# One 8 KB run per partition for the expert matrices, and the row list loaded one job ahead on GpSimd

## The chip, the core and the metric

The kernel runs on one core of a Trainium2 chip. The core has a matrix engine (TensorE, PE, with its weight loads shown as PEld), VectorE (DVE), ScalarE (ACT), GpSimd (POOL) and SyncE (SP), which here issues transfers only. Sixteen DMA engines move data between the chip's memory (HBM) and the on-chip memory of 128 partitions (SBUF). The metric is the time of one execution on the device in microseconds. Host work before the launch, such as laying out inputs anew, is not in it.

## What is computed

Two layers over 1024 latent and 256 context tokens of width 1024: a modulated attention sub-layer with three mixers, then a mixture of 32 SwiGLU experts. The change touches the second part alone:

```python
def hier_moe(h, w_rg, w_re, w_gate, w_up, w_down):
    ...                      # top-1 group of 4, then top-2 of its 8 experts, weights w
    order = jnp.argsort(flat_e)
    tok = order // TOP_K
    sizes = jnp.bincount(flat_e, length=N_EXPERTS).astype(jnp.int32)
    xs = h[tok]
    a = lax.ragged_dot(xs, w_gate, sizes)      # 1024 -> 512
    u = lax.ragged_dot(xs, w_up, sizes)        # 1024 -> 512
    y = lax.ragged_dot(jax.nn.silu(a) * u, w_down, sizes)   # 512 -> 1024
    y = y * w.reshape(-1)[order][:, None].astype(y.dtype)
    return jax.ops.segment_sum(y, tok, num_segments=n)
```

All tensors are float32. The first layer routes 1280 tokens, the second only the 1024 latent ones.

## The kernel before

A layer is four stages, each a block of programs, one for each engine: projection, attention, merge, experts. The experts stage routes the tokens, runs the experts in `run_experts`, and combines the results.

**Jobs.** `run_experts` deals the work in jobs. A job is up to 128 token rows of one expert; an expert with more rows gets more jobs. The number of jobs is data-dependent (`load_count`); the trace shows 35 in the first layer and 38 in the second. Each engine runs its own program over the jobs with a hardware loop (`Fori`), and semaphores alone tie the engines together.

**Weights.** For every job, SyncE loads the expert's three matrices, each 2 MB, in two halves of 1 MB into `raw[GATE]`, `raw[UP]` and `raw[DOWN]` (`load`, L2352; the source is written by `expert_half`, L2272). A partition's 2048 floats of a half are four rows of 512 for gate and up, and two rows of 1024 for down: since row k*128+p goes to partition p, its pieces lie 128 rows apart in HBM. A half is loaded again as soon as it has been split.

**Splitting.** The matrices are split into a rounded part and a rest, and each product is three passes. ScalarE writes the rounded part of both halves (`split`, L2410: L2415). VectorE subtracts to get the rest (L2519) for the halves of gate and up and the first half of down. GpSimd does the second half of down (`rest_of_down`, L2391: L2394). `wait_split` (L2334) is the wait for them, on TensorE and on SyncE before it reloads the half.

**TensorE** does in job g: gate (24 matmuls, L2566), up (24), the transposes of the rows of job g+1 (8, L2558), the down products of job g-1 (24, L2580), and the transposes of the hidden rows of job g (4, L2602).

**Rows.** GpSimd fetches the rows of job g+2 in `gather` (L2374): it waits until the gather before has landed, loads the list of 128 row numbers (`index`, one buffer, L2381), waits for it, waits until TensorE has transposed the rows of job g+1 (`xt`), and issues the indirect DMA that fills `x` (one buffer, L2386). After it, in the same iteration, comes `rest_of_down(g)`.

**VectorE's order** in job g (`body`, L2527) is: the two halves of gate for g+1, `hidden` of g (L2534), the rest of the transposed rows of g+1 (`rows_lo`, L2524), the two halves of up for g+1, the rest of hidden (L2539), first half of down. TensorE's gate products of g+1 wait for `rows_lo`. **ScalarE's order** (`body`, L2431) is: SiLU of g (L2435), gate of g+1, rows of g+1 (L2421), up of g+1, the result of g-1 and its store to `ye` (512 KB), hidden of g (L2443), down of g.

Of the kernel before, what the change touches and what calls it, by code (L numbers as in the profile page):

```python
# [17 lines left out]
P = 128  # L18
# [10 lines left out]
DEPTH, D, SEQ, CTX = 2, 1024, 1024, 256  # L29
# [13 lines left out]
NG, EG, NE, EH = 4, 8, 32, 512  # L43
# [22 lines left out]
def later(g, lag):  # L66


    return not isinstance(g, int) or g >= lag


def take_waits(eng, taken):


    eng.sem_inc(taken.sem, 1)
# [2196 lines left out]
def expert_half(io, l, e, n, half):  # L2272

    w = io[("w_exp_gate", "w_exp_up", "w_exp_down")[n]]
    rows = w.shape[2] // 2
    return w[l, e, half * rows:(half + 1) * rows, :].rearrange("o (k p) n -> p (o k) n", p=P)


def run_experts(nc, io, scr, l, nq, st, inner, ident, jobs, starts, more_jobs, r, scat, raw, raw_in,
# [5 lines left out]
    def sb(name, shape, dt=F32):  # L2285
        return st.sb(name, shape, dt, inner)
# [4 lines left out]
    w = [sb(f"w_{n}", [P, 2, 2, 2048], F32R) for n in ("gate", "up", "down")]  # L2291
# [23 lines left out]
    two = sb("two", [P, 2 * nq, NE])  # L2315
# [7 lines left out]
    def load_count(eng):  # L2323
        eng.wait_ge(counted.sem, counted.done(0))
        return eng.value_load(more_jobs[0:1, 0:1], min_val=0, max_val=J - NE) + NE
# [17 lines left out]
    with nc.Block() as block:  # L2343
# [27 lines left out]

        @block.gpsimd
        def _(pool):
            def gather(g):  # L2374
                if later(g, 1):
                    pool.wait_ge(x_in.sem, x_in.done(g - 1))
                if isinstance(g, int):
                    start = g * T
                else:
                    start = pool.value_load(starts[0:1, ds(g, 1)], min_val=0, max_val=NE * T - P)  # L2380
                pool.dma_start(index[:, :], scr["token_of"][ds(start, P), :]).then_inc(i_in.sem, 16)  # L2381
                pool.wait_ge(i_in.sem, i_in.done(g))
                if later(g, 1):
                    pool.wait_ge(xt.sem, xt.done(g - 1))
                take_waits(pool, taken)
                pool.indirect_dma_start(  # L2386
                    out=x, out_offset=None, in_=scr["h2"],
                    in_offset=bass.IndirectOffsetOnAxis(ap=index[:, :].bitcast(U32), axis=0)
                ).then_inc(x_in.sem, 16)

            def rest_of_down(g):  # L2391
                pool.wait_ge(w_hi[DOWN].sem, w_hi[DOWN].done(g * 2 + 1))
                take_waits(pool, taken)
                pool.tensor_tensor(w[DOWN][:, 1, 1, :], raw[DOWN][:, 1, :], w[DOWN][:, 0, 1, :].bitcast(F32),  # L2394
                                   ALU.subtract).then_inc(w_lo_pool.sem, 1)
            pool.wait_ge(scat.sem, scat.done(2 * nq - 1))
            gather(0)
            gather(1)
            n_jobs = load_count(pool)
            gather(2)  # L2400
            rest_of_down(0)
            with pool.Fori(1, n_jobs - 2) as g:
                gather(g + 2)
                rest_of_down(g)
            rest_of_down(n_jobs - 2)
            rest_of_down(n_jobs - 1)

# [275 lines left out]
def laid_out(inputs):  # L2683
# [3 lines left out]
    w = np.asarray(inputs["w_in"])  # L2687
# [6 lines left out]
    w_ada = [np.asarray(w).T.reshape(N_MOD * KD, P, D) for w in np.asarray(inputs["w_ada"])]  # L2694
    b_ada = [np.asarray(b).reshape(N_MOD * KD, P) for b in np.asarray(inputs["b_ada"])]
    two = 2 * KD
    return {"w_ada_rows0": np.concatenate([w_ada[0][two:], w_ada[1][:two]]), "w_ada_rows1": w_ada[1][two:],
            "b_ada_columns0": np.concatenate([b_ada[0][two:], b_ada[1][:two]]).T, "b_ada_columns1": b_ada[1][two:].T,
            "c_rows": np.concatenate([np.asarray(inputs["c"]).reshape(1, D), np.asarray(inputs["c_ctx"]).reshape(1, D)]),
            "w_router": np.ascontiguousarray(router.reshape(DEPTH, KD, P, NG + NE).transpose(0, 2, 1, 3)),  # L2700
# [51 lines left out]
```

## Time and profile before

| | us |
|---|---|
| median of 3 runs (4990.33 to 4995.63) | 4991.43 |
| the profiled execution | 4994.57 |
| its span, first to last instruction | 4993.0 |

| engine | busy us | share of the span |
|---|---|---|
| PE | 4550.5 | 91% |
| PEld | 3782.1 | 76% |
| DVE | 3299.8 | 66% |
| ACT | 2467.8 | 49% |
| POOL | 1194.9 | 24% |

Busy time is the union of an engine's instructions; ends of matmuls are modelled, so a busy TensorE is not one at its peak. The page cuts the span in 40 slices of 124.8 us. The two runs of expert jobs take from 1920 to 2570 us and from 4233 to 4940 us; in their inner slices the page gives a DMA share in tenths of 9 and 397 GB/s. The mean granted TensorE clock of the whole execution is 0.958 of full speed, and 1.00 in the inner part of the job loops.

### The profile page before, as it was taken

To read this page: it belongs to the slowest core of one execution; us is meant where nothing else is said; L and a number is where in the kernel's file an instruction comes from. 1 tells how busy PE (TensorE), PEld (TensorE's weight loads), DVE (VectorE), ACT (ScalarE), POOL (GpSimd) and SP (SyncE) were. 2 spreads that over 40 slices of the span, in tenths; PEclk is the share of its full clock that TensorE was granted. 3 is DMA by queue.
4 is the path that set the end of the run, shared out by engine and by line. 5 is a ranking of instruction groups with operands and counts; after the bars stand their busy time and mean duration, and the time that the engine had idled before them with its cause. 6 is when DMAs were issued, how large, how long until landed. Compare 5 with 4: busy or idle time off the path is not lost. (4 is left out here: it accounts for less than half of the span.)

```text
span 4993.0 us, 75967 instructions
## 1 busy us (share of the span) xinstructions
PE 4550.5 (91%) x25973; PEld 3782.1 (76%) x25973; DVE 3299.8 (66%) x5272; ACT 2467.8 (49%) x3056; POOL 1194.9 (24%) x921
## 2 busy tenths in 40 slices
PE   6999998899999897999967999999999987999995
PEld 4887877777878875887746878888877866778774
DVE  6653667676776567777777636677755436877776
ACT  3223555564233315777743226565633222777774
POOL 3650004400000013333334630053000001333333
PEclk8999999999999998999988999999999988999998
DMA  5645344264554566999995544353555345999998
GB/s 189 201 129 120 73 86 105 105 174 150 209 197 167 212 209 260 397 397 397 397 359 194 169 134 99 73 132 98 119 195 213 124 162 176 385 397 397 397 397 331
DMA packets 581798, 1088.92 MB, mean 218 GB/s; under 512 B 111876, under 2 KB 265380, under 8 KB 578552
## 3 DMA queue, kind: packets, MB, share of 16 engines
q1 hardware_dynamic: 531952, 919.40, 54.8%
q0 software_dynamic: 36272, 119.42, 6.4%
q10 hardware_dynamic: 13400, 47.85, 2.4%
q8 instruction: 102, 1.67, 0.1%
q14 instruction: 72, 0.59, 0.0%
HBM read 903.12 MB, written 183.43 MB: 218 GB/s over the span
## 5 line engine op out<-in xcount | busy, mean ns | idle before, releaser
L1817 PE MATMUL merge_acc<-ahead_wide,merge_w_split 128*128 128x512 f32 (+1 forms) x2880 | 638.3, 376 | 18.2 <-DMA ahead_wide<-hT 14.5
L1817 PEld LDWEIGHTS merge_acc<-ahead_wide,merge_w_split 128*128 128x128 f32 x2880 | 504.7, 190 | 126.6 <-issue 17.1
L665 PE MATMUL project_proj_acc<-ahead_wide,project_hT 128*128 128x512 f32 x2280 | 562.1, 399 | 1.9 <-DVE ahead_wide L486 0.9
L2519 DVE TENSOR_TENSOR experts_w_gate<-experts_raw_gate,experts_w_gate 128x2048 fp32r<-128x2048 f32 x146 | 362.0, 2484 | 298.0 <-ACT experts_w_gate L2415 297.9
L665 PEld LDWEIGHTS project_proj_acc<-ahead_wide,project_hT 128*128 128x128 f32 x2280 | 426.5, 191 | 91.7 <-DVE project_hT L516 3.8
L2394 POOL TENSOR_TENSOR experts_w_down<-experts_raw_down,experts_w_down 128x2048 fp32r<-128x2048 f32 x73 | 354.5, 4856 | 515.2 <-ACT experts_w_down L2415 515.2
L2566 PE MATMUL experts_gate_acc<-experts_w_gate,experts_rowsT 128*128 128x512 f32 x1752 | 433.1, 403 | 13.3 <-DVE experts_rowsT L2524 7.0
L981 DVE TENSOR_REDUCE attend_stat<-attend_scores 128x1 f32<-128x1280 f32 (+2 forms) x288 | 305.8, 1062 | 207.6 <-PE attend_scores L882 204.0
L2580 PE MATMUL experts_result_acc<-experts_w_down,experts_hiddenT 128*128 128x512 f32 x1752 | 430.2, 401 | 12.2 <-DVE experts_w_down L2519 12.2
L2566 PE MATMUL experts_up_acc<-experts_w_up,experts_rowsT 128*128 128x512 f32 x1752 | 420.7, 395 | 0.0
L2566 PEld LDWEIGHTS experts_gate_acc<-experts_w_gate,experts_rowsT 128*128 128x128 f32 x1752 | 327.6, 190 | 102.5 <-issue 22.9
L2580 PEld LDWEIGHTS experts_result_acc<-experts_w_down,experts_hiddenT 128*128 128x128 f32 x1752 | 327.0, 190 | 86.4 <-issue 12.6
L2566 PEld LDWEIGHTS experts_up_acc<-experts_w_up,experts_rowsT 128*128 128x128 f32 x1752 | 329.2, 188 | 79.6
L2415 ACT CAST experts_w_gate<-experts_raw_gate 128x2048 fp32r<-128x2048 f32 x146 | 279.0, 1914 | 215.6 <-DMA experts_raw_gate<-in_w_exp_gate_dram 196.7
L919 ACT COPY attend_probsT<-attend_scores 128x1024 f32<-128x1024 f32 (+1 forms) x288 | 216.6, 752 | 340.4 <-PE attend_scores L849 340.4
L1285 POOL TENSOR_TENSOR ahead_rows<-ahead_rows,attend_b_stat 128x640 f32<-128x640 f32 (+1 forms) x72 | 122.5, 1701 | 882.5 <-DVE attend_b_stat L1238 882.5
L2519 DVE TENSOR_TENSOR experts_w_up<-experts_raw_up,experts_w_up 128x2048 fp32r<-128x2048 f32 x146 | 327.4, 2284 | 1.1 <-ACT experts_w_up L2415 1.1
L1826 PE MATMUL merge_acc<-merge_yT,merge_w_split 128*128 128x512 f32 (+1 forms) x1440 | 320.1, 371 | 0.0
L2415 ACT CAST experts_w_up<-experts_raw_up 128x2048 fp32r<-128x2048 f32 x146 | 278.8, 1913 | 54.0 <-DMA experts_raw_up<-in_w_exp_up_dram 54.0
L931 ACT ACTIVATE attend_probs<-attend_scores,attend_stat 128x1280 f32<-128x1280 f32 (+2 forms) x288 | 284.8, 989 | 29.9 <-DVE attend_stat L989 14.1
L1826 PEld LDWEIGHTS merge_acc<-merge_yT,merge_w_split 128*128 128x128 f32 x1440 | 250.6, 187 | 53.3
L1646 ACT CAST merge_w_split<-ahead_rows 128x1536 fp32r<-128x1536 f32 x120 | 177.0, 1475 | 226.2 <-DMA ahead_rows<-in_w_merge_dram 118.1
(258 smaller groups left out, 8310.0 us busy)
## 6 DMA issues: line engine op xcount, KB each, us to landing
experts_raw_gate<-in_w_exp_gate_dram SPq DMA_DIRECT2D x146, 1024.0 KB, 14.0
experts_raw_up<-in_w_exp_up_dram SPq DMA_DIRECT2D x146, 1024.0 KB, 12.8
experts_raw_down<-in_w_exp_down_dram SPq DMA_DIRECT2D x146, 1024.0 KB
ahead_rows<-in_w_merge_dram SPq DMA_DIRECT2D x120, 768.0 KB, 6.0
merge_mod_w_ada<-in_w_ada_rows_dram POOLq DMA_DIRECT2D x80, 512.0 KB, 3.6
qk<-project_staged SPq DMA_DIRECT2D x74, 512.0 KB, 3.2
ye<-ahead_rows ACTq DMA_DIRECT2D x73, 512.0 KB, 6.3
attend_keys<-qk SPq DMA_DIRECT2D x96, 320.0 KB, 5.7
```

What stands on the lines that cost most here:

```text
L665: m = pe.matmul(acc[g % 2][:, :], hT[:, a, q * KP + k, t * P:(t + 1) * P], w_split[n % SLOTS][:, c, k, :], start=(q == 0 and i == 0 and k ...
L919: act.copy(probsT[b][:, 0:n, :], scores[b][:, 0:n * P].rearrange("p (j n) -> p j n", n=P)).then_inc(ca.sem, 1)
L931: act.activation(probs[b][:, 0:sx.n * P], scores[b][:, sx.cols], ACT.Exp, scale=SCORE_SCALE, bias=stat[:, s % 4, 1:2], accum_out=stat[:, s ...
L981: dve.tensor_reduce(stat[:, k, 0:1], scores[b][:, sx.cols], AX.X, ALU.max).then_inc(mx.sem, 1)
L1646: act.copy(w_split[b][:, 0, :, :], w_raw[b][:, :, :]).then_inc(wh.sem, 1)
L1817: m = pe.matmul(acc[:, b, 0:w], w_split[b][:, a, k, :], hT[:, x, k, 0:w], start=(i == 0 and k == 0), stop=(i == 2 and k == KD - 1))
L1826: m = pe.matmul(acc[:, 3 + b, 0:w], w_split[b][:, a, KD + k, :], yT[:, x, b * KB + k, 0:w], start=(i == 0 and k == 0), stop=(i == 2 and k ...
L2394: pool.tensor_tensor(w[DOWN][:, 1, 1, :], raw[DOWN][:, 1, :], w[DOWN][:, 0, 1, :].bitcast(F32), ALU.subtract).then_inc(w_lo_pool.sem, 1)
L2415: act.copy(w[n][:, 0, half, :], raw[n][:, half, :]).then_inc(w_hi[n].sem, 1)
L2519: dve.tensor_tensor(w[n][:, 1, half, :], raw[n][:, half, :], w[n][:, 0, half, :].bitcast(F32), ALU.subtract).then_inc(w_lo[n].sem, 1)
L2566: m = pe.matmul(acc[:, :], xT[:, a, half * (KD // 2) + k, :], w[n][:, c, half, k * EH:(k + 1) * EH], start=(half == 0 and i == 0 and k == ...
L2580: m = pe.matmul(acc_y[:, c0 * 512:(c0 + 1) * 512], hT[:, a, half * (HK // 2) + k, :], w[DOWN][:, c, half, k * D + c0 * 512:k * D + (c0 + 1 ...
```

## The change

There are two edits.

**Layout.** The host lays each half of each expert matrix out by partition: what partition p receives stands in one piece of 2048 floats (8 KB). `expert_half` describes it so. What lands in SBUF is the same as before, element for element; every product and every split is unchanged.

**Order on GpSimd.** `gather` is cut in two. `load_index(g)` waits for the landing of gather g-1 and issues the load of the list; `gather(g)` waits for the list and issues the indirect DMA. In the loop, iteration g now gathers the rows of job g+2, then loads the list of job g+3, then does `rest_of_down(g)`. The wait for the landing of gather g+2 thereby stands in front of `rest_of_down(g)`. The loop is one iteration shorter, and one gather and one subtraction stand behind it.

```diff
@@ expert_half
     rows = w.shape[2] // 2
-    return w[l, e, half * rows:(half + 1) * rows, :].rearrange("o (k p) n -> p (o k) n", p=P)
+    return w[l, e, half * rows:(half + 1) * rows, :].rearrange("o (p k) n -> p (o k n)", p=P)
@@ run_experts, gpsimd
-            def gather(g):
+            def load_index(g):
                 if later(g, 1):
                     pool.wait_ge(x_in.sem, x_in.done(g - 1))
...
                 pool.dma_start(index[:, :], scr["token_of"][ds(start, P), :]).then_inc(i_in.sem, 16)
+
+            def gather(g):
                 pool.wait_ge(i_in.sem, i_in.done(g))
                 if later(g, 1):
                     pool.wait_ge(xt.sem, xt.done(g - 1))
...
             pool.wait_ge(scat.sem, scat.done(2 * nq - 1))
+            load_index(0)
             gather(0)
+            load_index(1)
             gather(1)
             n_jobs = load_count(pool)
+            load_index(2)
             gather(2)
+            load_index(3)
             rest_of_down(0)
-            with pool.Fori(1, n_jobs - 2) as g:
+            with pool.Fori(1, n_jobs - 3) as g:
                 gather(g + 2)
+                load_index(g + 3)
                 rest_of_down(g)
+            gather(n_jobs - 1)
+            rest_of_down(n_jobs - 3)
             rest_of_down(n_jobs - 2)
             rest_of_down(n_jobs - 1)
@@ laid_out
+    def by_partition(name):
+        w = np.asarray(inputs[name])
+        rows, n = w.shape[2:]
+        halves = w.reshape(DEPTH, NE, 2, rows // (2 * P), P, n).transpose(0, 1, 2, 4, 3, 5)
+        return np.ascontiguousarray(halves).reshape(DEPTH, NE, rows, n)
+
+    return {"w_exp_gate": by_partition("w_exp_gate"), "w_exp_up": by_partition("w_exp_up"),
+            "w_exp_down": by_partition("w_exp_down"),
```

The order of instructions changes on GpSimd alone. Its job loop before, from the loop's entry to its branch; `experts_index` is the list, `ahead_rows` holds the rows `x`, `experts_w_down` the split down matrix, and the ISA rows carry waits and register work:

```order
L2402 ISA
L2380 ISA
L2380 TENSOR_LOAD experts_starts
L2380 ISA x2
L2381 REGISTER_ALU
L2381 DMA experts_index<-token_of 128x1
L2382 ISA
L2386 DMA ahead_rows<-h,experts_index 128x1024
L2392 ISA
L2394 TENSOR_TENSOR experts_w_down<-experts_raw_down,experts_w_down 128x2048
L2402 ISA
L2402 COMPARE_AND_BRANCH
```

In the changed kernel the same loop reads (L2386 to L2388 are `gather`, L2380 and L2381 `load_index`, L2396 the subtraction):

```order
L2408 ISA
L2386 REGISTER_ALU
L2388 DMA ahead_rows<-h,experts_index 128x1024
L2380 ISA
L2380 TENSOR_LOAD experts_starts
L2380 ISA x2
L2381 REGISTER_ALU
L2381 DMA experts_index<-token_of 128x1
L2394 ISA
L2396 TENSOR_TENSOR experts_w_down<-experts_raw_down,experts_w_down 128x2048
L2408 ISA
L2408 COMPARE_AND_BRANCH
```

The load of the list moved from in front of the gather to behind it, and is still in front of the subtraction. On GpSimd ahead of the loop, from the gather of job 1 to the subtraction of job 0, before:

```order
L2386 DMA ahead_rows<-h,experts_index 128x1024
L2325 TENSOR_LOAD experts_more_jobs
L2325 ISA x2
L2381 DMA experts_index<-token_of 128x1
L2386 DMA ahead_rows<-h,experts_index 128x1024
L2394 TENSOR_TENSOR experts_w_down<-experts_raw_down,experts_w_down 128x2048
```

and in the changed kernel:

```order
L2388 DMA ahead_rows<-h,experts_index 128x1024
L2325 TENSOR_LOAD experts_more_jobs
L2325 ISA x2
L2381 DMA experts_index<-token_of 128x1
L2388 DMA ahead_rows<-h,experts_index 128x1024
L2381 DMA experts_index<-token_of 128x1
L2396 TENSOR_TENSOR experts_w_down<-experts_raw_down,experts_w_down 128x2048
```

One more load of the list (that of job 3) stands between the gather of job 2 and the subtraction of job 0. On SyncE every load keeps its place; only its shape changes, from 128x4x512 (gate, up) and 128x2x1024 (down) to 128x2048.

## Rows read from the trace of the kernel before

**Rows 1.** The page: DMA busy tenths and GB/s in 40 slices.

```profile
DMA  5645344264554566999995544353555345999998
GB/s 189 201 129 120 73 86 105 105 174 150 209 197 167 212 209 260 397 397 397 397 359 194 169 134 99 73 132 98 119 195 213 124 162 176 385 397 397 397 397 331
```

**Rows 2.** Windows: busy us of each engine (x count), PEclk, DMA share, GB/s.

```profile
1200.00:1350.00 150.00, 150.00 (x644) 120.21 (x644) 111.17 (x149) 41.84 (x44) 11.20 (x22) 1.00 0.56 210
2000.00:2500.00 500.00, 496.97 (x2278) 400.44 (x2278) 373.21 (x216) 382.23 (x270) 170.42 (x82) 1.00 1.04 397
```

**Rows 3.** Waits, 2000 to 2500 us: total us, times, longest.

```profile
DVE experts_w_gate L2519 <- ACT experts_w_gate L2415: 117.0, 53, 4.2
ACT experts_w_gate L2415 <- DMA experts_raw_gate<-in_w_exp_gate_dram: 79.9, 54, 2.2
...
PE experts_gate_acc L2566 <- DVE experts_rowsT L2524: 0.3, 2, 0.2
```

**Rows 4.** Timeline of one middle job: start us, us, engine, line, operation [idle before].

```profile
2207.46 1.92 ACT L2415 CAST experts_w_gate<-experts_raw_gate 128x2048 fp32r<-128x2048 f32 x1 [0.80 <-DMA experts_raw_gate<-in_w_exp_gate_dram]
...
2209.41 2.29 DVE L2519 TENSOR_TENSOR experts_w_gate<-experts_raw_gate,experts_w_gate 128x2048 fp32r<-128x2048 f32 x1 [0.21 <-ACT experts_w_gate L2415]
...
2211.62 0.68 DVE L2534 TENSOR_TENSOR ahead_rows<-ahead_rows,experts_up_acc 128x512 f32<-128x512 f32 x1
2212.22 1.22 DVE L2524 TENSOR_TENSOR experts_rowsT<-experts_rowsT_acc,experts_rowsT 128x1024 fp32r<-128x1024 f32 x1
...
2212.75 1.00 POOL L2386 DMA_INDIRECT ahead_rows<-h,experts_index  x1 [5.19 <-DMA experts_index<-token_of]
...
2213.57 5.85 PE L2566 MATMUL experts_gate_acc<-experts_w_gate,experts_rowsT 128*128 128x512 f32 x24
```

**Rows 5.** SiLU of each job (L2435): xcount, first and last start; then two starts.

```profile
L2435 ACT ACTIVATE ahead_rows<-experts_gate_acc x34: 588/600/612, 1944.5 to 2553.1; 128x512 f32<-128x512 f32 x34
...
L2435 ACT ACTIVATE ahead_rows<-experts_gate_acc x30: 588/599/612, 2017.1 to 2553.1; 128x512 f32<-128x512 f32 x30
...
L2435 ACT ACTIVATE ahead_rows<-experts_gate_acc x37: 584/598/622, 4258.5 to 4922.7; 128x512 f32<-128x512 f32 x37
...
1962.63 0.60 ACT L2435 ACTIVATE ahead_rows<-experts_gate_acc 128x512 f32<-128x512 f32 x1 [0.49 <-PE experts_gate_acc L2566]
...
1980.74 0.60 ACT L2435 ACTIVATE ahead_rows<-experts_gate_acc 128x512 f32<-128x512 f32 x1 [0.19 <-PE experts_gate_acc L2566]
```

**Rows 6.** Modulation: weight loads waiting for 8 KB-run DMAs; then DMA queues' shares.

```profile
11.74 0.11 PEld L179 LDWEIGHTS modulation_mod_acc<-modulation_w_ada,modulation_sT 128*2 128x2 f32 x8 [2.33 <-DMA modulation_w_ada<-in_w_ada_dram]
14.17 0.11 PEld L179 LDWEIGHTS modulation_mod_acc<-modulation_w_ada,modulation_sT 128*2 128x2 f32 x8 [2.32 <-DMA modulation_w_ada<-in_w_ada_dram]
...
q1 hardware_dynamic: 895, 6.41, 94.9%
...
q1 hardware_dynamic: 14461, 33.80, 89.2%
q10 hardware_dynamic: 864, 3.15, 7.8%
```

**Rows 7.** Timeline of an early job, and landing of the row gathers there.

```profile
1961.52 2.28 DVE L2519 TENSOR_TENSOR experts_w_down<-experts_raw_down,experts_w_down 128x2048 fp32r<-128x2048 f32 x1
...
1962.33 5.97 POOL L2394 TENSOR_TENSOR experts_w_down<-experts_raw_down,experts_w_down 128x2048 fp32r<-128x2048 f32 x1 [2.65 <-ACT experts_w_down L2415]
...
1965.07 7.58 DVE L2519 TENSOR_TENSOR experts_w_gate<-experts_raw_gate,experts_w_gate 128x2048 fp32r<-128x2048 f32 x2 [1.27 <-ACT experts_w_gate L2415]
...
1968.04 1.03 PE L2558 MATMUL experts_rowsT_acc<-experts_ident,ahead_rows 128*128 128x128 f32 x8
...
1973.17 1.21 DVE L2524 TENSOR_TENSOR experts_rowsT<-experts_rowsT_acc,experts_rowsT 128x1024 fp32r<-128x1024 f32 x1
...
1974.86 1.42 PE L2566 MATMUL experts_gate_acc<-experts_w_gate,experts_rowsT 128*128 128x512 f32 x5
...
DMA to landing us min/median/max: 7.3/7.7/8.9
```

More of the change, by code:

```diff
@@ L2696, in laid_out @@
     two = 2 * KD
-    return {"w_ada_rows0": np.concatenate([w_ada[0][two:], w_ada[1][:two]]), "w_ada_rows1": w_ada[1][two:],
+    def by_partition(name):
[5 more added lines that the diff above has]
+            "w_exp_down": by_partition("w_exp_down"),
+            "w_ada_rows0": np.concatenate([w_ada[0][two:], w_ada[1][:two]]), "w_ada_rows1": w_ada[1][two:],
             "b_ada_columns0": np.concatenate([b_ada[0][two:], b_ada[1][:two]]).T, "b_ada_columns1": b_ada[1][two:].T,
```

## The prediction, made before the changed kernel ran

> **What bounds the kernel now.** I read the page's 40 slices first. In the inner slices of the two job loops the DMA digit is 9 and the rate is the same number in slice after slice, 397 GB/s [rows 1]. A resource that shows one constant rate for 500 us is a candidate for the bound. The window over 2000 to 2500 us gives a DMA share of 1.04 (transfers overlap on an engine, so it can exceed 1), and TensorE busy 496.97 of 500 us at full clock [rows 2]. Both look full, so busy time can't decide.
>
> The waits decide. ScalarE waits for gate halves 79.9 us in these 500 us, and VectorE waits for ScalarE's gate casts 117.0 us, while TensorE shows 0.3 us of waiting [rows 3]. The timeline of one job shows how this reaches TensorE: the second gate half lands at 2207.46, ScalarE casts it until 2209.38, VectorE subtracts until 2211.70, then does `hidden` and the row rest until 2213.44, and TensorE's next gate products start at 2213.57, 0.13 us later [rows 4]. The chain starts with a transfer and ends at TensorE; TensorE's gap is small and partly hidden by the modelled ends of its matmuls.
>
> How much the transfers cost is read from the job period. In the first layer 30 SiLUs stand between 2017.1 and 2553.1 us: 29 periods of 18.48 us. Earlier, before the backlog has grown, SiLUs stand at 1962.63 and 1980.74: 18.11 us [rows 5]. A job moves six halves of 1.049 MB, a gather and a store of 0.524 MB each, 7.34 MB. At 397 GB/s that is 18.49 us, just the slow period. The fast one is TensorE's own: 150 us of pure matmul work in the merge stage hold 644 of them [rows 2], 0.233 us each, so a job's 72 take 16.8 us, which leaves 1.3 us for 12 transposes of 128 columns. So the job loop runs at the DMA's pace, 0.37 us a job above TensorE's.
>
> **Part 1, the layout.** In each half a partition's four pieces of 2 KB (gate, up) or two of 4 KB (down) become one of 8 KB; bytes, number of loads and their order stay. What 8 KB runs give is shown by the modulation stage, which loads its 1 MB pieces in such runs: TensorE, waiting for each, gets them at 11.74 and 14.17 us, 2.43 us apart, or 431 GB/s [rows 6]. Six halves then take 14.6 us. Gather and store keep 4 KB rows: ScalarE's queue, which carries just such stores, moved 3.15 MB in 7.8% of 100 us of all engines, 404 GB/s [rows 6], so 1.05 MB takes 2.6 us. Sum 17.2 us a job, 0.9 below TensorE's 18.11. Even at 410 GB/s for everything it is 17.9. Hence TensorE becomes the bound, and only the difference between 18.48 and 18.11 is won.
>
> Counted over the rows: the first layer's 34 SiLUs from 1944.5 to 2553.1 are 33 periods, 608.6 us; at 18.11 they are 597.6, which saves 11.0. The second layer's 37 from 4258.5 to 4922.7 are 36 periods, 664.2 us against 652.0, which saves 12.2 [rows 5]. **Together 23.2 us.** The jobs before and the tail behind hold no wait for a weight transfer on TensorE's path, so I count nothing there (0 to 2 us less is possible).
>
> A rule of the Trainium skill speaks against this part. What the rows show: 397 GB/s held for 500 us [rows 2], and 431 in 8 KB runs [rows 6]. "DMA: Bandwidth & Descriptors", section "Where 436 GB/s comes from", says that for transfers from HBM to SBUF the HBM side binds, at some 358 GB/s for a core. If a limit of HBM made the 397, run length would change nothing. Both measured rates lie above the page's figure, so the trace does not agree with it here; I keep the case as a rival.
>
> **Part 2, the list ahead.** Removed: GpSimd's wait of 5.19 us for the list before each gather [rows 4]. It buys nothing on the path, since the gathered rows are not waited for by TensorE in this window [rows 3]; the gather only starts some 5 us earlier. Added: in front of the subtraction (L2394), the wait for the landing of the gather just issued, a register load and the issue of the list load (0.6 us). Queued behind it on GpSimd is the subtraction, and for that wait TensorE's second down half and SyncE's reload of that half, with all of SyncE's later loads.
>
> Is the cover long enough? I use the early job, which already runs at 18.11 us [rows 7]. GpSimd is free at 1968.30, TensorE's transposes of the job's rows end at 1969.07, so the gather can be issued at 1969.2. The next subtraction was ready to start at 1962.33 + 18.1 = 1980.5. Between them lie 11.3 us. Gathers landed 7.3 to 8.9 us after issue [rows 7]; with 0.7 us for the list load that is 8.0 to 9.6. Cover is left, 1.7 to 3.3 us. The subtraction has another microsecond, for it didn't begin work at 1962.33: it took 5.97 us, and its normal length, 4.7, fits only if it began when VectorE's down split ended at 1963.80. Value taken: 0, with 0 to 5 us for the two loop starts, where the list of job 3 comes before the subtraction of job 0.
>
> The same rows show what is late next. With TensorE as the bound, GpSimd's subtraction and VectorE's gate split meet: the split's two halves took 7.58 us instead of two times 2.29, ending with GpSimd's end plus two halves. Down split end 1963.80, GpSimd 4.5, gate split 4.35, `hidden` and row rest 1.73 end at 1974.38; TensorE took up gate at 1974.86. So the spare time in that loop is 0.4 us, and this is where a late subtraction would show.
>
> **Rivals.**
> Partial: the DMA comes to about 401 to 406 GB/s only, or the GpSimd-VectorE loop takes 0.1 to 0.2 us of each job. Then 18.2 to 18.3 us a job, saving 8 to 17 us: 4974 to 4983. For it: 4 KB rows stay in the mix and the loop's spare time is small. Against it: the early jobs had that same collision and ran at 18.11.
> Unchanged: the 397 is a limit of the memory and not of the pieces, 4991. Against it stand the 431.
> Slower: the gather lands too late. Each of the 16 engines serves several queues, and the gather's 8 rows on each are interleaved with weight pieces. Modulation's pieces took 0.949 x 16 us x 16 engines / 895 = 0.27 us on average, the job loop's 0.892 x 100 x 16 / 14461 = 0.10 us [rows 6]. One more such piece in front of each row adds 0.17 x 8 = 1.4 us to the landing, which the cover still holds (10.3 at most of 10.6 us). With four in front it adds 5.4 us: landing at up to 14.3, subtraction late by 3.7 less the spare 1.4, some 2.3 us in each of 69 jobs, 159 less 23, about 5127. It decides from about 12 us between issue and landing; at 12.5 us it costs 0.5 us a job, 35 us, and the time is 5003. By "Queues, rings and completion order" on the same page an engine takes the queues in turn and finishes a packet before it switches. By that rule one weight packet stands in front of each row, which is the 1.4 us; no row shows packets of two queues side by side.
>
> **How the numbers follow.** The profiled execution took 4994.57 us, 3.1 above the median. 4994.57 - 23.2 = 4971.4 in its own terms, 4968.2 against the median. Forecast (18.11 us a job; 4963 to 4974): 0.71. Partial: 0.14. Unchanged: 0.07. Slower: 0.08, most of it between 4995 and 5040. The range 4963 to 4985 leaves out unchanged and slower, 15 in 100, and little else. A measurement of this kernel tells about 0.2%, 10 us, from no change: faster is below 4981.4, that is the forecast and most of partial, 0.82; same 0.10; slower 0.08.
>
> **What would show it.** Right: SiLU periods of 18.1 us through both loops; ScalarE no longer waiting for gate halves (under 10 us in 500); a DMA share below 1 with about 405 GB/s, which is now demand and not limit; VectorE's gate split at 7 to 8 us for two halves in every job; the subtraction released by ScalarE's down cast. Wrong: ScalarE still waiting for gate halves at 18.4 us and 397 GB/s (unchanged); the list load or the subtraction released by the gather's landing, with TensorE waiting for down or the row rest (slower).

## The result, and the profile after

The changed kernel took 5023.43 us, the median of 6 runs (5009.5 to 5052.73), beside 4991.97 us for the kernel before (6 runs, 4989.63 to 4996.25): ratio 1.0075, 95% interval 1.006 to 1.0091. It is slower, and its own runs lie six times as far apart as those of the kernel before (43.2 us against 6.6). The profiled execution is its fastest: 5009.5 us, span 5008.0. The prediction, 4968.2, is 55 us away and on the other side.

The page of the kernel after: rates of the 40 slices. They answer to [rows 1].

```profile
GB/s 189 200 127 120 80 86 99 118 167 157 199 191 164 227 202 276 406 399 395 406 327 208 152 144 93 76 117 112 129 189 189 123 179 212 358 365 388 406 395 326
```

In place of one constant number the inner slices now read 358 to 406. The DMA is no longer the bound: where all goes well it moves 406 GB/s, about what the jobs ask for at TensorE's pace (7.34 MB in 18.11 us is 405), and in the second loop (slices 35 to 37) it moves less than before.

The SiLU of each job, after: count, first and last start, for the two loops. Before, the same 35 stood from 1929.4 to 2553.1 and the 38 from 4243.4 to 4922.7 us.

```profile
L2444 ACT ACTIVATE ahead_rows<-experts_gate_acc x35: 597/599/622, 1927.6 to 2547.7; 128x512 f32<-128x512 f32 x35
...
L2444 ACT ACTIVATE ahead_rows<-experts_gate_acc x38: 586/598/602, 4235.5 to 4937.1; 128x512 f32<-128x512 f32 x38
```

The first loop went from 623.7 to 620.1 us, 3.6 less; the second from 679.3 to 701.6, 22.3 more. The other stretches together gave 3.7 back, which makes the 15.0 us by which the spans differ. Single periods of the second loop are 19.1 to 20.9 us (one 23.6) for its jobs 2 to 16, and 18.1 to 18.7 after that. In the first loop two of three are 18.1 or 18.2 and the others reach 19.2.

The stretches after (TensorE, its weight loads, VectorE, ScalarE, GpSimd busy us, then granted clock, DMA share, GB/s), against [rows 2]:

```profile
2000.00:2500.00 500.00, 496.76 (x2295) 402.44 (x2294) 458.21 (x217) 383.49 (x273) 201.34 (x83) 1.00 1.00 401
4250.00:4550.00 300.00, 278.11 (x1248) 218.91 (x1247) 252.38 (x120) 214.38 (x151) 117.90 (x46) 0.99 0.94 362
4550.00:4900.00 350.00, 348.44 (x1609) 282.62 (x1608) 318.89 (x155) 267.04 (x190) 136.93 (x57) 1.00 1.00 401
```

Between 4250 and 4550 us TensorE stands still for 22 us, and the DMA has idle time (share 0.94). The waits of this stretch (us in total, times, longest) name what holds it:

```profile
POOL experts_index L2381 <- issue: 158.2, 14, 12.0
...
ACT experts_w_gate L2424 <- DMA experts_raw_gate<-in_w_exp_gate_dram: 29.5, 19, 2.6
...
PEld experts_result_acc L2589 <- POOL experts_w_down L2396: 19.1, 15, 2.2
PE experts_result_acc L2589 <- POOL experts_w_down L2396: 12.3, 11, 1.8
```

TensorE waits for the second down half, which is GpSimd's subtraction; the kernel before had no such wait between 2000 and 2500 us. GpSimd in turn stands up to 12.0 us ahead of the list load (L2381). The page writes "issue" there, but what the list load waits for in the program is one thing, the landing of the gather issued just before, and behind it the register load for the list's address (L2380). From the landing to the issue of the list load pass 1.3 us in the first loop and 1.4 us here (medians). The timelines of GpSimd (start, duration, and in brackets the idle time before) show both conditions of the loop. First two good jobs, then two bad ones:

```profile
2206.27 1.24 POOL L2388 DMA_INDIRECT ahead_rows<-h,experts_index  x1 [1.79 <-PE experts_rowsT_acc L2567]
2216.72 0.57 POOL L2381 DMA_DIRECT2D experts_index<-token_of  x1 [9.21 <-issue]
2217.31 4.96 POOL L2396 TENSOR_TENSOR experts_w_down<-experts_raw_down,experts_w_down 128x2048 fp32r<-128x2048 f32 x1
2224.38 3.11 POOL L2388 DMA_INDIRECT ahead_rows<-h,experts_index  x1 [2.11 <-PE experts_rowsT_acc L2567]
```

```profile
4321.49 1.90 POOL L2388 DMA_INDIRECT ahead_rows<-h,experts_index  x1 [1.11 <-DMA experts_index<-token_of]
4335.39 0.58 POOL L2381 DMA_DIRECT2D experts_index<-token_of  x1 [12.00 <-issue]
4335.98 5.17 POOL L2396 TENSOR_TENSOR experts_w_down<-experts_raw_down,experts_w_down 128x2048 fp32r<-128x2048 f32 x1
4341.63 2.55 POOL L2388 DMA_INDIRECT ahead_rows<-h,experts_index  x1 [0.48 <-issue]
```

In a good job GpSimd waits 2.11 us for TensorE's transposes at the end of its round; gather to gather is 18.11 us. In a bad one the spare is gone. From 4321.49 to 4341.63 nothing in the round waits for TensorE: 13.90 us from gather to list load, 0.59 to the subtraction, 5.17 for it, 0.48 more, 20.14 us in all. The subtraction isn't alone in the last part of it, though. The list is on its way at the same time. This one landed 5.4 us after its issue, at 4340.7, and the gather was issued 0.9 us later. So it is in most rounds here. In 12 of the 16 gathers from 4240 to 4545 us the gather starts 0.8 to 0.9 us after the list's landing, and in the other 4 within 0.2 us of the subtraction's end. The list loads of this stretch (issue in ns, then time to landing in us, min/median/max):

```profile
L2381 POOL DMA_DIRECT2D experts_index<-token_of x16: 550/571/577, 4241.2 to 4534.6; - x16
...
DMA to landing us min/median/max: 3.7/5.2/5.6
```

The chain of a bad round is thus gather, landing (12.4 us in the median, below), list load (1.4), landing of the list (5.2), next gather (0.9): 19.9 us, with the subtraction beside the list's transfer and nearly as long. TensorE follows one step behind; it waits in its down products:

```profile
4336.48 3.05 PE L2589 MATMUL experts_result_acc<-experts_w_down,experts_hiddenT 128*128 128x512 f32 x12
4341.21 3.06 PE L2589 MATMUL experts_result_acc<-experts_w_down,experts_hiddenT 128*128 128x512 f32 x12 [1.68 <-POOL experts_w_down L2396]
```

The last piece is the gather's own time. First 2000 to 2500 us, then 4240 to 4545 us: issue in ns and time from the start of the issue to the landing in us, each min/median/max. [Rows 7] had 7.3/7.7/8.9 for the early jobs; between 2000 and 2500 us the kernel before has 6.9/7.0/7.2.

```profile
L2388 POOL DMA_INDIRECT ahead_rows<-h,experts_index x27: 988/1887/3107, 2005.9 to 2482.5; - x27
...
DMA to landing us min/median/max: 8.6/10.1/12.1
...
L2388 POOL DMA_INDIRECT ahead_rows<-h,experts_index x16: 1743/2524/3062, 4247.2 to 4540.9; - x16
...
DMA to landing us min/median/max: 9.5/12.4/13.1
```

The issue gets longer where VectorE is at work. The gather issued at 4321.49 ends at 4323.39, 0.86 us after the end of this half of the gate split, which was running when the issue began:

```profile
4317.21 5.32 DVE L2528 TENSOR_TENSOR experts_w_gate<-experts_raw_gate,experts_w_gate 128x2048 fp32r<-128x2048 f32 x1 [1.44 <-ACT experts_w_gate L2424]
```

The same holds for all gathers of both kernels. Of the 146, 74 were issued while VectorE subtracted a half of the weights (4 before, 70 after), and each of them ended 0.84 to 0.94 us after that half did. The other 72 took 0.97 to 1.00 us.

So the theory after the profile: 8 KB pieces would have given the forecast gain, but they and the new order together make the gather land later than the cover allows, and GpSimd's gather, its landing, the list load and what follows it close into one round. The rivals: the new order alone costs it; the 8 KB pieces cost by themselves, whatever the order.

### The profile page after: what moved, and what is told of

Read it like the earlier page. It is cut to its first block and busy times, and to the rows that moved or that the text cites. A ratio compares the mean times of both kernels' runs of the same rounds, so it can differ in the third digit from the quotient of the medians.

```text
span 5008.0 us, 75951 instructions
## 1 busy us (share of the span) xinstructions
PE 4543.1 (91%) x25973; PEld 3773.7 (75%) x25973; DVE 3491.9 (70%) x5272; ACT 2464.9 (49%) x3056; POOL 1259.8 (25%) x921
## 5 line engine op out<-in xcount | busy, mean ns | idle before, releaser
L2528 DVE TENSOR_TENSOR experts_w_gate<-experts_raw_gate,experts_w_gate 128x2048 fp32r<-128x2048 f32 x146 | 557.0, 3846 | 140.2 <-ACT experts_w_gate L2424 140.2
L1817 PEld LDWEIGHTS merge_acc<-ahead_wide,merge_w_split 128*128 128x128 f32 x2880 | 505.3, 190 | 127.6 <-issue 18.1
L2575 PE MATMUL experts_gate_acc<-experts_w_gate,experts_rowsT 128*128 128x512 f32 x1752 | 433.7, 404 | 18.2 <-DVE experts_rowsT L2533 17.8
L2589 PEld LDWEIGHTS experts_result_acc<-experts_w_down,experts_hiddenT 128*128 128x128 f32 x1752 | 325.8, 190 | 104.1 <-POOL experts_w_down L2396 19.1
L2396 POOL TENSOR_TENSOR experts_w_down<-experts_raw_down,experts_w_down 128x2048 fp32r<-128x2048 f32 x73 | 354.9, 4861 | 68.4 <-ACT experts_w_down L2424 67.4
L1463 POOL DMA_DIRECT2D merge_mod_w_ada<-in_w_ada_rows_dram x80 | 42.3, 529 | 961.4 <-DVEq L1487 606.0
```

The lines of the kernel that those rows point to most:

```text
L1817: m = pe.matmul(acc[:, b, 0:w], w_split[b][:, a, k, :], hT[:, x, k, 0:w], start=(i == 0 and k == 0), stop=(i == 2 and k == KD - 1))
L2528: dve.tensor_tensor(w[n][:, 1, half, :], raw[n][:, half, :], w[n][:, 0, half, :].bitcast(F32), ALU.subtract).then_inc(w_lo[n].sem, 1)
L2575: m = pe.matmul(acc[:, :], xT[:, a, half * (KD // 2) + k, :], w[n][:, c, half, k * EH:(k + 1) * EH], start=(half == 0 and i == 0 and k == ...
L2589: m = pe.matmul(acc_y[:, c0 * 512:(c0 + 1) * 512], hT[:, a, half * (HK // 2) + k, :], w[DOWN][:, c, half, k * D + c0 * 512:k * D + (c0 + 1 ...
```

## The experiments

All ratios are against the kernel before on the same chip.

**One part at a time.** `a1_layout_only` is the kernel before with the 8 KB layout and GpSimd's old order.

```
-    return w[...].rearrange("o (k p) n -> p (o k) n", p=P)
+    return w[...].rearrange("o (p k) n -> p (o k n)", p=P)
```

> The kernel before with the 8 KB layout alone; GpSimd's order is the old one. Theory A (the wait): the changed kernel loses because GpSimd waits 9 to 13 us for a gather to land, in front of its subtraction, so a chain of gather, landing, list load and subtraction becomes longer than a job. Then the layout alone gives what was forecast for it, 18.1 us a job, 4966 to 4972 us. Theory B (the pieces): 8 KB pieces in the queues cost by themselves, by slower gathers and stores, whatever the order; then this one is above 4995 too. Theory C (the collision): TensorE's pace makes GpSimd's and VectorE's subtractions exclude each other, and that alone costs some tenths of a us a job; then 4975 to 4995, with TensorE waiting for the row rest in most jobs.

Measured: 5020.82 us (5014.6 to 5028.51), ratio 1.006, interval 1.0043 to 1.0076. `a2_order_only` is the changed kernel in the old pieces, so only the list's load is moved.

> The changed order on GpSimd with the old pieces of 2 and 4 KB. Theory A: the gather starts some 5 us earlier and lands 7 to 10 us later; a job takes 18.5 us and the subtraction is ready 13.8 us after the one before, so the wait is covered: 4988 to 4996 us, no change from before. If gathers take over 12 us here too, the order alone costs as in the changed kernel, 5010 or more. Theory B: no change, 4992. Theory C: no change, since the transfers still set the pace.

Measured: 4993.47 us (4985.63 to 4997.31), ratio 1.0005, interval 0.9996 to 1.0015: no change, 18.5 us a job. So the order alone costs nothing that can be measured, and the 8 KB pieces lose with either order. My first theory, that the added wait alone is the cause, falls. But the layout alone shows waits of the same kind, between 2000 and 2500 us:

```profile
POOL ahead_rows L2386 <- DMA experts_index<-token_of: 165.9, 26, 7.2
...
POOL experts_index L2381 <- issue: 71.8, 26, 3.6
...
PEld experts_rowsT_acc L2558 <- DMA ahead_rows<-h,experts_index: 32.4, 26, 2.1
```

In each of 26 jobs TensorE's transposes wait for the gathered rows, up to 2.1 us. The landing is there 9.6/11.1/12.4 us (min/median/max) instead of 7.0. And in each of 26 jobs GpSimd stands idle ahead of the list load, up to 3.6 us, with its subtraction done. It waits for the landing of the gather before, as `gather` says it must, and the list load comes 1.3 us after that landing. One round of it:

```profile
2073.09 1.00 POOL L2386 DMA_INDIRECT ahead_rows<-h,experts_index  x1 [7.03 <-DMA experts_index<-token_of]
...
2084.29 0.56 POOL L2381 DMA_DIRECT2D experts_index<-token_of  x1 [2.42 <-issue]
2092.04 1.18 POOL L2386 DMA_INDIRECT ahead_rows<-h,experts_index  x1 [7.19 <-DMA experts_index<-token_of]
```

This gather landed after 9.9 us, the list load was issued 1.3 us later and landed after 6.9 us, and 0.8 us behind it stands the next gather: 18.95 us. So the old order is closed by the same chain, gather, landing, list, landing, gather, with the subtraction off to the side. In the kernel before the chain was 7.0 + 1.3 + 5.0 + 0.8 = 14.1 us of a job's 18.48 and never showed. There the list load followed right behind the subtraction.

`a3_list_behind` is the changed kernel with the list load behind the subtraction:

```
                 gather(g + 2)
-                load_index(g + 3)
                 rest_of_down(g)
+                load_index(g + 3)
```

> The changed kernel with the list load of the next job behind the subtraction in place of in front of it (in the loop and before it); the gather still comes first, and its landing is now waited for behind the subtraction. Theory A: the loss is gone, 18.1 us a job, 4965 to 4972 us, with gathers that still land after 8 to 13 us. Theory B: above 4995. Theory C: 4975 to 4995, as in the kernel with the layout alone.

Measured: 5019.54 us (5009.21 to 5031.69), ratio 1.0069, interval 1.0053 to 1.0086; gathers land after 9.5/10.7/12.0 us. Taking the list out from in front of the subtraction doesn't help. In each of 27 jobs between 2000 and 2500 us the list load is issued 1.3 us after the gather's landing, later than the end of the subtraction, and its own landing (5.9 us in the median) stands ahead of the next gather. The subtraction can be outside the round and the round is still too long.

**Smaller pieces.** `a4_pieces_4kb` is the changed kernel with two 4 KB pieces for each partition and half.

```
-    return w[...].rearrange("o (p k) n -> p (o k n)", p=P)
+    return w[...].rearrange("o (j p k) n -> p (o j) (k n)", j=2, p=P)
```

> The changed kernel with two pieces of 4 KB for each partition and half, instead of one of 8 KB. Theory A: what counts is how long a gather takes to land; with pieces half as long in its way it lands after 8 to 11 us, so fewer jobs or none are over the limit of some 12 us: 4970 to 4990 us. If the landing doesn't get shorter, 5010 to 5040 as with 8 KB. Theory B: half the loss, about 5005.

Measured: 4972.59 us (4964.21 to 4981.03), ratio 0.9969, interval 0.9955 to 0.9983: faster, and 64 of 71 periods are 18.1 us. `b1_4kb_old_order` has the same pieces in GpSimd's old order.

> The kernel before with the expert matrices laid out for two 4 KB pieces for each partition and half, and GpSimd in its old order (subtraction of job g, then the list of job g+2, then its gather). The runs so far: old pieces with the new order 1.0005 of the time before, 8 KB pieces 1.006 with the old order and 1.0075 with the new one, 4 KB pieces with the new order 0.9969. Theory A (what costs is how late the gathered rows land, and the old order puts the list's 5 to 6 us and the gather's 8 to 10 us one behind the other, after the subtraction): with gathers that land in 8 to 10 us the old chain subtraction 4.7 + list 5.8 + gather issue 1 to 2 + landing 8 to 10 = 20 to 22 us does not close into a loop by itself (the next subtraction doesn't wait for the landing), but the transposes meet the rows late in some jobs, so 18.1 to 18.5 us a job and 4973 to 4985 us. Theory B (the order is of no account at 4 KB): the same as with the new order, 4972 us, and no wait of the transposes for rows. Theory C (the order is what gains): no better than before, 4985 to 4995 us.

Measured: 4973.14 us (4969.0 to 4975.2), ratio 0.996, interval 0.9944 to 0.9975. Both orders do equally well. Its stretch from 2000 to 2500 us, columns as above:

```profile
2000.00:2500.00 500.00, 500.00 (x2322) 407.29 (x2321) 437.00 (x222) 388.22 (x276) 180.70 (x83) 1.00 1.02 405
```

TensorE is busy all the time, at 405 GB/s. This is the state that I had forecast, so it needs longer pieces than before, but not 8 KB, and not the list one job ahead.

**The round cut open, with 8 KB pieces.** The test between "the landing, by the round" and "8 KB pieces by themselves" leaves the pieces as they are and cuts the chain from the landing to the list. `b2_two_lists` gives the list a second buffer: GpSimd copies the list that has arrived into the buffer the gather reads, starts the next load at once, gathers, and subtracts.

```
             def load_index(g):
                 if later(g, 1):
-                    pool.wait_ge(x_in.sem, x_in.done(g - 1))
+                    pool.wait_ge(ic.sem, ic.done(g - 1))
...
+            def copy_index(g):
+                pool.wait_ge(i_in.sem, i_in.done(g))
+                if later(g, 1):
+                    pool.wait_ge(x_in.sem, x_in.done(g - 1))
...
+                pool.tensor_copy(index[:, :], index_next[:, :]).then_inc(ic.sem, 1)
...
             with pool.Fori(1, n_jobs - 3) as g:
-                gather(g + 2)
+                copy_index(g + 2)
                 load_index(g + 3)
+                gather(g + 2)
                 rest_of_down(g)
```

> The changed kernel, 8 KB pieces as they are, with a second list buffer: GpSimd copies the list that has arrived into the one that the gather reads (128 numbers), starts the load of the next list at once, gathers, and subtracts. Neither the load of a list nor the subtraction waits any more for the gathered rows of the same round to land. Theory A (the loss of the changed kernel is the closed loop on GpSimd of gather issue, landing 12 to 13 us, list issue 0.6 us, subtraction 4.7 us, longer than TensorE's 18.11 us; the 8 KB pieces do harm only through the landing): with the loop cut the jobs go at 18.1 us in both layers, as with 4 KB pieces, 4967 to 4976 us, and the gather may still take 10 to 13 us to land. Theory B (8 KB pieces cost by something else, such as less bandwidth or weights that arrive unevenly): the jobs stay at 18.5 to 20 us, 5005 to 5030 us. Theory C (the copy on GpSimd waits for VectorE or makes it wait): some 0.3 to 1 us a job on top of theory A, 4980 to 5005 us, with VectorE or GpSimd named in TensorE's waits.

Measured: 4973.84 us (4968.84 to 4980.14), ratio 0.9963, interval 0.995 to 0.9977. All jobs but the first and last of each loop take 18.1 us. Three instructions of GpSimd, in the stretch of the bad jobs above:

```profile
4330.61 1.01 POOL L2397 DMA_INDIRECT ahead_rows<-h,experts_index  x1 [0.30 <-issue]
4339.53 4.81 POOL L2405 TENSOR_TENSOR experts_w_down<-experts_raw_down,experts_w_down 128x2048 fp32r<-128x2048 f32 x1 [7.91 <-ACT experts_w_down L2438]
4344.28 2.26 POOL L2390 COPY experts_index<-experts_index_next 128x1 int32<-128x1 int32 x1
```

The subtraction is again released by ScalarE's cast, after 7.91 us of idling: nothing in this round is late, although the gather still needs up to 11.3 us to land (2000 to 2500 us). This kernel also issues its gathers in 1.02 us, so they land somewhat earlier than in the changed kernel, 9.5 against 10.1 us in the median, and that alone would help. But 6 of its 73 gathers took more than 10.6 us to land, and none of these 6 rounds was over 18.2 us. In `a1_layout_only` it was 41 of 73, and all 41 rounds were over 18.25. The kernel is 50 us faster than the changed one (5023.43), which is what the round costs, and 8 KB pieces cost nothing that can be measured once the round is open.

Two controls. `b3_two_lists_4kb` is the same with 4 KB pieces, `c1_two_lists_old_pieces` with the old ones.

> The kernel with the second list buffer and the copy, with two 4 KB pieces for each partition and half. Theory A (landing only matters through the loop, and at 4 KB pieces nearly all jobs are at 18.11 us already): as the 4 KB kernel with one list, 4970 to 4975 us, at best 1 to 3 us less from the few jobs at 18.2 to 18.5 us. Theory B (8 KB pieces are worse by themselves): as theory A here, but clearly ahead of the 8 KB kernel with two lists. Theory C (the copy collides with VectorE): 4980 to 5005 us.

Measured: 4976.98 us (4973.67 to 4979.07), ratio 0.9968, interval 0.9956 to 0.9981.

> The second list buffer and the copy alone, with the expert matrices in the old 2 and 4 KB pieces: the control for the kernel with two lists and 8 KB pieces, which took 0.9963 of the time before. Theory A (the loop on GpSimd was the loss of the 8 KB pieces only, and the gain over the kernel before comes from the DMA queues' faster pieces): the jobs stay at 18.5 us, bound by the DMA queues at 397 GB/s, 4985 to 4996 us, ratio 0.999 to 1.001. Theory B (the second list buffer gains by itself, whatever the pieces): 18.1 us a job, 4970 to 4978 us.

Measured: 4995.31 us (4988.74 to 4998.48), ratio 1.0008, interval 0.9998 to 1.0018. The second buffer gains nothing by itself; with the old pieces the DMA bounds the loop at 397 GB/s and some 18.5 us a job. These three kernels differ only in their pieces, and GpSimd issues the gather behind the same work, in 1.02 us. So they measure what the pieces do to the landing (the old pieces with a job 2% longer than the other two). In this order the old pieces, 4 KB, 8 KB, all 2000 to 2500 us:

```profile
DMA to landing us min/median/max: 7.0/7.5/7.8
```

```profile
DMA to landing us min/median/max: 7.6/8.1/9.1
```

```profile
DMA to landing us min/median/max: 8.8/9.5/11.3
```

What moves beside the rows can be counted. For one gather of each kernel (issued at 2374.41, 2119.38 and 2206.85 us), this is the queue of the weights (packets, MB, share of the 16 engines) while the gather's 128 rows came in, which took 2.7, 3.3 and 4.6 us:

```profile
q1 hardware_dynamic: 257, 0.55, 53.6%
```

```profile
q1 hardware_dynamic: 210, 0.83, 63.1%
```

```profile
q1 hardware_dynamic: 152, 1.11, 62.9%
```

With 8 KB pieces fewer packets pass beside the rows, but they hold twice the bytes.

**A delay put in.** `c2_4kb_list_twice` is `a4_pieces_4kb` (all jobs well) with each list loaded twice, one load behind the other.

```
                 pool.dma_start(index[:, :], ...).then_inc(i_in.sem, 16)
+                pool.wait_ge(i_in.sem, i_in.done(g * 2))
...
+                pool.dma_start(index[:, :], ...).then_inc(i_in.sem, 16)
```

> The 4 KB kernel with the changed order (one list buffer; 4972.6 us, jobs of 18.1 us), with the suspected delay put in on purpose: each list is loaded twice, one load behind the other, so that the subtraction stands some 5 us later behind the landing of the gathered rows. Theory A (the loop gather issue, landing, list, subtraction on GpSimd sets the time of a job as soon as it is longer than TensorE's 18.11 us, whatever the size of the pieces): 1 to 2 + 9.4 + 0.6 + 4.9 + 0.6 + 4.7 = 21.2 to 22.2 us a job, over 72 jobs 220 to 295 us more, 5190 to 5270 us, with TensorE waiting for the second half of the down weights by GpSimd. Theory B (the 8 KB pieces themselves were the loss, the loop is not): nothing or little, 4972 to 4985 us.

Measured: 5346.66 us, one run. TensorE's waits between 2000 and 2500 us, then a round of GpSimd:

```profile
PEld experts_result_acc L2592 <- POOL experts_w_down L2399: 84.2, 21, 6.5
```

```profile
2199.97 0.54 POOL L2384 DMA_DIRECT2D experts_index<-token_of  x1 [5.36 <-DMA experts_index<-token_of]
2200.52 5.13 POOL L2399 TENSOR_TENSOR experts_w_down<-experts_raw_down,experts_w_down 128x2048 fp32r<-128x2048 f32 x1
2205.79 2.89 POOL L2391 DMA_INDIRECT ahead_rows<-h,experts_index  x1
2217.89 0.57 POOL L2381 DMA_DIRECT2D experts_index<-token_of  x1 [9.21 <-issue]
2223.48 0.54 POOL L2384 DMA_DIRECT2D experts_index<-token_of  x1 [5.01 <-DMA experts_index<-token_of]
```

The round is closed: 2199.97 to 2223.48, 23.5 us, and the job follows it (from first to last SiLU 23.1 us a job in both loops). It confirms the mechanism with small pieces, and misses my number: I had 21.2 to 22.2 us a job, 5190 to 5270. The gather's issue took 2.9 us and not 1 to 2, the landing 10.6 us from the start of the issue and not 9.4, and between the landing and the next list load stand 1.3 us that I had at nothing. (I had also counted the issue twice, since the 9.4 begin with it.) The granted clock of TensorE was 0.93 between 2000 and 2500 us, where it was busy for 425 of 500 us; TensorE has no part in this round.

**A dose between.** `c3_down_in_4kb` is the changed kernel with down in 4 KB pieces, gate and up in 8 KB.

> The changed kernel with 8 KB pieces for gate and up and two 4 KB pieces for down: a dose between the two. The gather is issued about where the gate and up transfers of the next job start, and the down transfers come behind. Theory A (what counts is how large the pieces are that the gathered rows meet, and those are gate and up): landing 9.5 to 12 us as with 8 KB pieces everywhere, many jobs at 18.5 to 20 us, 4995 to 5025 us. Theory B (the down pieces matter as much, they are what the next round of the loop meets): in between, 4975 to 4995 us.

Measured: 5034.03 us (5009.25 to 5065.14), ratio 1.0092, interval 1.0052 to 1.0133; gathers land after 9.2/11.2/12.8 us. It is a miss above both ranges, and no better than 8 KB everywhere. The pieces that the gathered rows meet are gate's and up's. Of 4179 weight pieces that started between 2000 and 2500 us while gathered rows came in, 4061 were of 8 KB. So this run doesn't show what the down pieces do.

## Why the prediction was wrong

**The bound: right.** The loop before ran at the DMA's pace, 18.48 us a job, and TensorE's floor is 18.11. Four kernels (`a4_pieces_4kb`, `b1_4kb_old_order`, `b2_two_lists`, `b3_two_lists_4kb`) stand on that floor.

**Part 1, 23.2 us: right in mechanism and size, once the rows come in time.** From first to last SiLU `b2_two_lists` has 614.7 and 667.1 us where the kernel before had 623.7 and 679.3: 21.2 less. Its 4973.84 and the 4973.14 of `b1_4kb_old_order` lie in the forecast's own range, 4963 to 4974. The rate went to 405 GB/s as demand, as said. The rival of a limit of the memory (the Trainium skill, "DMA: Bandwidth & Descriptors", "Where 436 GB/s comes from", some 358 GB/s) is out: 406 GB/s stood for 500 us in `b2_two_lists`. What I did not ask is what larger weight pieces do to the other queue's gather in the old order; `a1_layout_only` shows it to be enough to lose.

**Part 2, "Value taken: 0": this step failed.** I put down GpSimd's wait of 5.19 us for the list as removed, and asked one thing of the gather's landing, whether the subtraction was covered. But the list load waits for that landing, in both orders, and the next gather waits for the list. The list's wait wasn't removed, it was put behind the landing. The prediction has no round of landing, list and next gather, and that round set the pace: landing + 1.3 to 1.4 + 5.2 + 0.9 us in the changed kernel, landing + 1.3 + 6.0 + 0.8 with the layout alone. It reaches TensorE's 18.11 at a landing of about 10.6 us in the new order and 10.0 in the old one. The terms of the sum were short as well:
- The list load, at 0.7 us. From the landing to the start of the subtraction it took 1.3 to 1.4 us until the list load is issued and 0.6 us for the issue, 2.0 us together. That alone takes the cover for the landing from 10.6 to 9.3 us.
- The landing, 7.3 to 8.9 us, and 10.3 at most with 1.4 us for the pieces. The base was read in the old order, where the gather is issued in 0.99 us. The new order issues it some 5 us earlier, right behind the transposes, and there VectorE is in its gate split. With the old pieces the issue took 2.16 us (median) in `a2_order_only` and 1.02 in `c1_two_lists_old_pieces`, and the landing came after 8.6 and 7.5 us, 1.1 more in each. With 4 KB pieces the issue took 1.97 and 1.02, and the landing 9.4 and 8.1: about one more again. I had treated the earlier gather as free; it isn't. I had used the exclusion of GpSimd and VectorE for the subtraction in the next paragraph, and not for the gather's issue.
- The effect of the pieces, 1.4 us, was measured at 2.0 in the median (7.5 to 9.5) and 3.5 at the maximum (7.8 to 11.3).
- Together: 7.5 + 1.1 + 2.0 = 10.6 in the median. The trace has 8.6/10.1/12.1 in the first loop, just where the round begins to be too long.

**Where the 1.4 us went short.** The records have the queue and the time of every packet. From the first to the last of a gather's 128 rows it took 2.6, 3.4 and 4.5 us (2, 4 and 8 KB pieces, medians of 2000 to 2500 us), and for each row 1.8, 1.5 and 1.1 weight pieces started in that time, of about 0.085, 0.16 and 0.31 us each. With 8 rows on each of 16 engines that makes 8 x (1.1 x 0.31 - 1.8 x 0.085) = 1.5 us between 2 and 8 KB, and 0.2 rows of the result's store for each gathered row add 0.3, of 1.9 measured. So one piece for each row was about right with 8 KB. What was short is the length of a piece, 0.31 us and not 0.27, the store, and the spread. In the longest case, 6.2 us, 1.5 weight pieces and 0.7 store rows passed for each row. That the Trainium skill would also give one piece for each row was my misreading. By "DMA: Bandwidth & Descriptors", "Queues, rings and completion order", an engine drains a whole packet, typically some 9 to 17 descriptors, before it changes queues, so its packet isn't one piece. The records name no engine, so no run here shows that order.

**The rival "slower" was the right one, and the sign for it came true; its threshold, its chance and its price for one job did not hold.** It said that the gather decides from about 12 us, and that at 12.5 us the loss is 0.5 us in each of 69 jobs, 5003. The round shows that it decides from about 10.6 us. Measured between 4240 and 4545 us the landing was 12.4 us in the median, and the loss some 2 us a job (20.1 against 18.1), in the profiled run in 15 of 37 periods; 5009.5 us. That the two sums are alike is chance. A chance of 0.08 was too little where the worst landing stood 0.3 us below its cover (10.3 of 10.6) and two of the terms had not been measured in the new order.

**What none of the rivals had: a late round lengthens the landing.** I priced a late subtraction as so much in each job, less the spare. In the bad stretch the issue took 2.5 us against 1.9 in the first loop (medians), and for each gathered row 0.7 rows of the result's store came through, where most gathers of the first loop had none. At 4327.5 to 4333.2 us, while one gather's rows came in, the store's queue moved:

```profile
q10 hardware_dynamic: 120, 0.49, 20.9%
```

The landing went from 10.1 to 12.4 us. 0.6 of it is the issue, and 0.7 x 0.16 x 8 = 0.9 us is an estimate of what the store's rows take. The loop stays bad for 15 jobs and then drops back to 18.1. It would account for the spread of the runs, 43 us where the kernel before has 7. What makes it enter and leave that condition is not shown by any run here.

**Signs that I had named:** ScalarE's waits for gate halves fell to 8.5 us in 500 in the first loop, under the 10 that I had named, while the gain wasn't there; in the bad stretch they were 29.5 us in 300. That sign alone could not tell right from wrong. "The list load or the subtraction released by the gather's landing, with TensorE waiting for down" is what came. With the layout alone TensorE waited for the gathered rows instead.

## What to carry to other kernels

A transfer off the critical path has its own slack; before you speed up what shares the DMA engines with it, or move its issue, write down its largest time to landing and the work that must hide it. Then follow each buffer around until you come back to the same instruction. Here one buffer for the list and one for the rows closed the round gather, landing, list, landing, gather, and it was 4 us below the period before the change. If such a round's sum is within a few microseconds of the period, cut it with a second small buffer. The smallest step that gains is often enough: 4 KB pieces in the old order gave all that 8 KB pieces could, with nothing else changed.

## What the runs showed of the hardware

- Larger pieces on one queue delay another queue's small-row gather. With the same order and the same 1.02 us of issue it landed after 7.5, 8.1 and 9.5 us (2 and 4 KB, 4 KB, 8 KB pieces), and at worst after 7.8, 9.1 and 11.3. One weight piece took about 0.085, 0.16 and 0.31 us (2, 4, 8 KB).
- From 4 KB pieces on the 1 MB weight loads kept up with 405 GB/s of demand; with gate and up in 2 KB pieces the same loop held at 397.
- An indirect gather that GpSimd issues while VectorE subtracts a 128x2048 half (both inputs on chip) ends its issue 0.84 to 0.94 us after that half does, up to 3.1 us in all (74 gathers of the kernels before and after). Without a half running at its start it takes 0.97 to 1.00 us, and a half that begins later doesn't stretch it. The landing moves by as much.
- From the landing of a gather to the issue of the list load that waits for it pass 1.3 to 1.4 us on GpSimd, with one register load in it. The list of 128 numbers landed 5.0 us after its issue in the kernel before and up to 6.9 in `a1_layout_only`.
- GpSimd's copy of 128 numbers took 2.26 us in `b2_two_lists`. It cost nothing there, with 7.9 us of idling in the same round.
